# One transformer layer in fp32: dt's eight weight columns move into v's units, and the last four output tiles are shared among three engines

## The reference, cut to what matters

```
h = rms_norm(x, norm_mix_pre)
z, xbc, dt_raw, q, k, v = split(h @ w_in)        # 512, 1024, 8, 512, 512, 512 columns
dt = softplus(dt_raw + dt_bias)                  # per token and head
y_ssd = ssd_mixer(z, silu(conv(xbc)), dt, ...)   # running sums of dt * a in chunks of 128 tokens
y_diff = diff_attention(q, k, v, ...)
x = x + rms_norm(concat(y_ssd, y_diff) @ w_out, norm_mix_post)
x = x + rms_norm(cross_attention(rms_norm(x), rms_norm(mem)), norm_mem_post)
m = square(relu(rms_norm(x, norm_mlp_pre) @ w_up)) @ w_down
x = x + rms_norm(m, norm_mlp_post)
```

## Time and profile before

| | us |
|---|---|
| three runs, median (lowest to highest) | 1526.33 (1525.86 to 1528.11) |
| the profiled execution's own time | 1526.56 |
| its span | 1524.8 |
| PE busy | 1466.3 (96%) |
| DVE busy | 949.3 (62%) |
| ACT busy | 691.2 (45%) |
| GpSimd busy | 73.0 (5%) |
| HBM traffic, mean over the span | 116 GB/s |

### The profile page before, as it was taken

The page is one execution under the profiler, slowest core; times in us unless marked ns, Lnnn a source line. Parts: engine busy times, 40 slices in busy tenths (PEclk is TensorE's granted clock), DMA queues, the critical chain, the costliest instruction groups (busy, mean ns, idle before and its releaser), DMA issues. The chain is left out here.

```text
span 1524.8 us, 23241 instructions
## 1 busy us (share of the span) xinstructions
PE 1466.3 (96%) x8872; PEld 1287.9 (84%) x8872; DVE 949.3 (62%) x1658; ACT 691.2 (45%) x1473; POOL 73.0 (5%) x128
## 2 busy tenths in 40 slices
PE   7999999998998999999999989999999999999997
PEld 6889999996667999888999978888888788888885
DVE  4773465636886523711642588888777585557897
ACT  6314221225886523722642465544444464444442
POOL 1000000001001000100000234000000000000000
PEclk9999999999999999999999999999999999999999
DMA  8201111112001541011001242566443598766463
GB/s 308 65 28 42 28 29 29 29 42 84 1 1 56 160 159 43 29 56 43 14 29 56 98 135 80 180 208 219 152 152 125 195 341 285 243 227 193 155 231 110
DMA packets 99901, 177.68 MB, mean 117 GB/s; under 512 B 10576, under 2 KB 43472, under 8 KB 97744
## 3 DMA queue, kind: packets, MB, share of 16 engines
q1 hardware_dynamic: 94096, 152.05, 29.4%
q10 hardware_dynamic: 5696, 24.15, 5.0%
HBM read 138.42 MB, written 37.75 MB: 116 GB/s over the span
## 5 line engine op out<-in xcount | busy, mean ns | idle before, releaser
L1992 PE MATMUL ps<-wh,oph 128*128 128x256 f32 x1024 | 294.7, 288 | 3.2 <-DVE opl L1268 1.6
L1994 PE MATMUL ps<-wh,opl 128*128 128x256 f32 x1024 | 289.7, 283 | 0.0
L1993 PE MATMUL ps<-wl,oph 128*128 128x256 f32 x1024 | 289.7, 283 | 0.0
L1992 PEld LDWEIGHTS ps<-wh,oph 128*128 128x128 f32 x1024 | 196.2, 192 | 4.2 <-issue 2.0
L1993 PEld LDWEIGHTS ps<-wl,oph 128*128 128x128 f32 x1024 | 196.4, 192 | 0.1
L1994 PEld LDWEIGHTS ps<-wh,opl 128*128 128x128 f32 x1024 | 196.2, 192 | 0.0
L1992 PE MATMUL ps<-d_ring 128*128 128x512 f32 x448 | 174.7, 390 | 4.5 <-DVE d_ring L1877 4.5
L1993 PE MATMUL ps<-d_ring 128*128 128x512 f32 x448 | 174.4, 389 | 0.0
L1994 PE MATMUL ps<-d_ring 128*128 128x512 f32 x448 | 174.4, 389 | 0.0
L1255 DVE TENSOR_TENSOR wl<-raw,wh 128x1024 fp32r<-128x1024 f32 x60 | 73.1, 1223 | 91.8 <-ACT wh L741 91.1
L1183 ACT ACTIVATE d_ring<-left_raw 128x512 fp32r<-128x512 f32 x112 | 70.2, 627 | 98.0 <-PE ps L1994 76.9
(11 more groups left out here) (350 smaller groups left out, 2983.4 us busy)
## 6 DMA issues: line engine op xcount, KB each, us to landing
right_raw<-in_w_down_dram SPq DMA_DIRECT2D x128, 256.0 KB, 3.8
u_kept_s<-us SPq DMA_DIRECT2D x64, 256.0 KB, 2.8
left_raw<-u_kept_s SPq DMA_DIRECT2D x64, 256.0 KB, 2.9
w_blk<-in_w_up_blocks_dram ACTq DMA_DIRECT2D x14, 1024.0 KB, 6.0
left_raw<-u_kept_a SPq DMA_DIRECT2D x48, 256.0 KB, 3.1
raw<-in_w_in_dram SPq DMA_DIRECT2D x22, 512.0 KB, 3.7
u_kept_a<-u SPq DMA_DIRECT2D x24, 256.0 KB, 2.5
x_in<-in_x_dram SPq DMA_DIRECT2D x8, 512.0 KB, 9.2
```

The source lines that it names most:

```text
L1992: te.matmul(o, lh, rh, start=first, stop=False)
L1993: te.matmul(o, lh, rl, start=False, stop=False)
L1994: return te.matmul(o, ll, rh, start=False, stop=last)
```

## The change

**dt with v.** dt is no step of its own. The host lays the weights of dt and of v side by side in one tensor `w_vdt` of 520 columns, and v's two units have 260 columns each (`VC`). The slots of `wh`, `wl` and `raw` grow to 8 x 260 columns (`SLOT`). ACT evacuates each of v's first eight steps by two instructions: eight columns into `dt_tok`, 252 into `vt`. The loads, casts, products, evacuations and transposes of dt alone are gone. Softplus moves behind step n = 7 (`softplus` on ACT, `step_sizes` on DVE), the running sums to n = 10 and 11, and the SSD chunks to n = 12, 17, ..., 47. `silu_z` moves to the place of the rotary tables, so z's first step waits for `rope_done` in place of `ssd_b`, and the gate of each z tile waits for that tile's SSD output instead of all.

**The down stage.** PE waits for each of the last four chunks in turn. The multiplication of `c22_d` by the gain goes from DVE to GpSimd (`gain_last`). For tiles 4 to 6, ACT scales the second half by the tile's factor and GpSimd adds it to the residual (`finish_second`); DVE finishes the first half, one tile behind (`finish_half`). Tile 7 is finished by DVE alone. SP stores the last four tiles in halves of 512 columns, so 256 KB each.

```
-PROJ = [("xbc", 4, 4), ("dt", 2, 0), ("v", 8, 2), ("q", 8, 2), ("k", 8, 2), ("z", 8, 2),
+PROJ = [("xbc", 4, 4), ("v", 8, 2), ("q", 8, 2), ("k", 8, 2), ("z", 8, 2),
+VC = 260
+SLOT = KD * VC
-SSD_FIRST = {5 + 5 * c: c for c in range(NT)}
+SSD_FIRST = {n: c for c, n in enumerate(range(12, 12 + 5 * NT, 5))}
+C21_KEPT = {j: 16 + 2 * j + 1 for j in range(4)}
...
# SP
+            for j in range(4):
+                i, rows = 4 + j, slice((4 + j) * P, (5 + j) * P)
+                sp.wait_ge(finished, i + 1)
+                sp.dma_start(out[0][rows, 0:512], resid_d[:, i, 0:512]).then_inc(stored, 16)
+                if j < 3:
+                    sp.wait_ge(c22_p, 4 + j + 1)
+                else:
+                    sp.wait_ge(finished, NT + 1)
+                sp.dma_start(out[0][rows, 512:1024], resid_d[:, i, 512:1024]).then_inc(stored, 16)
...
# GpSimd
+            def gain_last(j):
+                pool.wait_ge(dn_kept, DN_KEPT["c22"] + j + 1)
+                g.tensor_tensor(c22_d[:, j, :], c22_d[:, j, :], gain_a[:, 512:1024], ALU.mult).then_inc(c22_p, 1)
+            def finish_second(j):
+                pool.wait_ge(dn_kept, C21_KEPT[j] + 1)
+                g.tensor_tensor(resid_d[:, 4 + j, 512:1024], c22_d[:, j, :], resid_d[:, 4 + j, 512:1024], ALU.add).then_inc(c22_p, 1)
...
+                if what == ("down", 4):
+                    for j in range(4):
+                        gain_last(j)
                 pow_step(what)
+                if what in (("down", 4), ("down", 5), ("down", 6)):
+                    finish_second(what[1] - 4)
...
# ACT, v's steps
+                    if u == 0:
+                        s.activation(dt_tok[:, i, :], ps[:, bank(g), 0:SSD_H], ACT.Copy, scale=scale).then_inc(dt_ev, 1)
+                        s.activation(vt[:, i, 0:VC - SSD_H], ps[:, bank(g), SSD_H:VC], ACT.Copy, scale=scale).then_inc(ev["v"], 1)
+                    else:
+                        s.activation(vt[:, i, VC - SSD_H:512], ps[:, bank(g), 0:VC], ACT.Copy, scale=scale).then_inc(ev["v"], 1)
...
+                if n == 7:
+                    softplus()
-                if n == 3:
+                if n == 11:
                     decays()
...
# ACT, the tail
                 s.activation(sq_d[:], c21_d[:, j, :], ACT.Square, accum_out=parts[:, j + 4, 0:1]).then_inc(dn_kept, 1)
+                if j < 3:
+                    act.wait_ge(c22_p, j + 1)
+                    act.wait_ge(rms_ready, POW[("down", j + 4)] + 1)
+                    s.activation(c22_d[:, j, :], c22_d[:, j, :], ACT.Copy,
+                                 scale=rms[:, COL[("down", j + 4)]:COL[("down", j + 4)] + 1]).then_inc(dn_kept, 1)
...
# DVE, v's steps and the tail
+                if n == 7:
+                    step_sizes()
+                if n == 11:
+                    running_sums()
+                if n == 12:
+                    chunk_ends()
...
-                    v.tensor_tensor(c22_d[:, r - 6, :], c22_d[:, r - 6, :], gain_a[:, 512:1024], ALU.mult).then_inc(gained, 1)
...
                 last_mean(j)
-                dve.wait_ge(gained, 9 + j)
-                finish(j + 4, y135_d[:, j, :], c22_d[:, j, :])
+                if j:
+                    dve.wait_ge(gained, 8 + j)
+                    finish_half(j + 3, 0, y135_d[:, j - 1, :]).then_inc(finished, 1)
+            dve.wait_ge(gained, 12)
+            finish_half(7, 0, y135_d[:, 3, :]).then_inc(finished, 1)
+            dve.wait_ge(c22_p, 4)
+            finish_half(7, 1, c22_d[:, 3, :]).then_inc(finished, 1)
...
# PE
-                if n == 0:
-                    dt_transpose()
-                if n == 3:
+                if n == 10:
                     sums_of_da()
...
-            pe.wait_ge(dn_lo, 2 * NC)
             for j in range(4):
                 for m in range(NC - ENDING, NC):
+                    pe.wait_ge(dn_lo, 2 * m + 2)
                     ins = down_chunk(m, j)
```

More of the change, by code:

```diff
@@ L647, in _ @@
                     store(m - 6 * NB - 2)
-            for i in range(4, NT):
-                store(i)
-            sp.wait_ge(stored, 16 * NT)
+            for j in range(4):
[7 more added lines that the diff above has]
+                sp.dma_start(out[0][rows, 512:1024], resid_d[:, i, 512:1024]).then_inc(stored, 16)
+            sp.wait_ge(stored, 16 * (NT + 4))
         @block.gpsimd
@@ L820, in _, with softplus @@
             silu(7)
[L821 to L829, removed]
+            def softplus():
+                act.wait_ge(small_loaded, N_SMALL)
+                act.wait_ge(dt_v, 1)
+                after(s.activation(dts[1][:], dts[0][:], ACT.Abs))
+                s.activation(dts[2][:], dts[1][:], ACT.Exp, scale=-1.0).then_inc(dt_s, 1)
+                act.wait_ge(dt_v, 2)
+                s.activation(dts[4][:], dts[3][:], ACT.Ln).then_inc(dt_s, 1)
+                s.activation(heads8[:, 1, :], heads8[:, 1, :], ACT.Exp).then_inc(dt_s, 1)
+                act.wait_ge(lam_s, 1)
+                s.activation(lam[:, 2:4], lam[:, 0:2], ACT.Exp).then_inc(dt_s, 1)
             def decays():
@@ new lines, in _, with running_sums @@
+            dt, e_cum, e_end, dt_end = dts[0], dts[4], dts[7], dts[2]
+            def running_sums():
+                dve.wait_ge(cum_done, 1)
+                cum, end = dts[5], dts[6]
+                v.tensor_copy(cum[:], ps[:, 4, 0:64].rearrange("p (c h) -> p c h", h=SSD_H)).then_inc(dv, 1)
+                v.tensor_copy(end[:], ps[:, 4, 64:128].rearrange("p (c h) -> p c h", h=SSD_H)).then_inc(dv, 1)
+                n_dv[0] += 2
+                dve.wait_ge(dv, n_dv[0])
+                after(v.tensor_scalar(ncum[:], cum[:], -1.0, None, ALU.mult))
+                v.tensor_tensor(dts[2][:], end[:], cum[:], ALU.subtract).then_inc(dt_v, 1)
@@ L1411, in heads, with chunk_ends @@
+            def chunk_ends():
+                dve.wait_ge(dt_s, 7)
+                after(v.tensor_tensor(lam[:, 4:5], lam[:, 3:4], lam[:, 2:3], ALU.subtract))
+                after(v.tensor_scalar(lam[:, 4:5], lam[:, 4:5], -LAMBDA_INIT, None, ALU.add))
+                after(v.tensor_tensor(dt_end[:], dt[:], dts[8][:], ALU.mult))
             def heads(a):
@@ L1904, in down_mean, with finish_half @@
                 mean(("down", i), D)
-            def finish(i, first, second):
+            def finish_half(i, half, part):
                 dve.wait_ge(rms_ready, POW[("down", i)] + 1)
@@ L1910, in finish @@
                 scale = rms[:, COL[("down", i)]:COL[("down", i)] + 1]
-                v.scalar_tensor_tensor(resid_d[:, i, 0:512], first, scale, resid_d[:, i, 0:512], ALU.mult, ALU.add)
-                v.scalar_tensor_tensor(resid_d[:, i, 512:1024], second, scale, resid_d[:, i, 512:1024],
-                                       ALU.mult, ALU.add).then_inc(finished, 1)
+                cut = slice(512 * half, 512 * half + 512)
+                return v.scalar_tensor_tensor(resid_d[:, i, cut], part, scale, resid_d[:, i, cut], ALU.mult, ALU.add)
+            def finish(i, first, second):
+                finish_half(i, 0, first)
+                finish_half(i, 1, second).then_inc(finished, 1)
             chunk_lo(0)
```

162 lines of the change are left out of this document (62 added, 100 removed).

## The result

The changed kernel takes 1517.31 us (median; 1513.65 to 1518.89), the kernel before, on the same chip in turns with it, 1528.11. The ratio is 0.9923 [0.9898, 0.9947]: by the ratio it is 11.8 us faster, with 8.1 to 15.6 inside the interval (the medians alone differ by 10.8). The forecast was 14.6 us less and a time of 1511.7, at most 1514.8. So the direction was right, and the median lies 2.5 us above the upper end of the range. Of the 5.6 us between 1511.7 and 1517.31, 1.8 are the kernel before, whose median was 1526.33 when the forecast was made and 1528.11 here; a range moved up by that would still end 0.7 us too low.

What follows compares the result with a forecast made beforehand. PE, busy for 96% of the span, was taken to bound the kernel, except in the tail. The terms -11.58 - 1.84 - 0.9 - 0.3 = -14.6 us took 1526.33 to 1511.7 us, range 1508.6 to 1514.8.

Steps and rivals of the forecast that it cites:

- Part A: Projections: dt's columns go into v's steps; dt's steps, transpose and a bank wait leave PE, -11.58 us in all.
- The wider product: v's 384 products: four more columns each, priced at 0.42 ns a column, +0.64 us.
- The lower end: v's 384 products: four more columns cost nothing, if a product doesn't feel them.
- The rival of a step to the price of 512 columns: v's products: 260 columns cost PE what 512 do, 41.3 us replace 0.64, ending at 1552.4 us; chance 0.03.
- 1.6 us as an upper end: v's 384 products: 4 ns more each, as dt's products showed, 1.6 us beyond the price by columns.
- B1: Last four chunks of the down stage: waits per chunk close PE's gap, -1.84 us, range -1.84 to +0.2.
- B2: Tail after PE's last products: shared among engines, DVE and GpSimd excluding each other, 13.9 us for 14.79, -0.9 us.
- The rival with no taking of turns: Tail: DVE and GpSimd don't hinder each other, tail 11.95 us, total 1509.8 us; chance 0.15.
- B3: End of the span: the last store is half as large, -0.3 us, range 0 to -0.65.

Runs made afterwards that it cites:

- e7: The changed kernel with a slot stride of 8,448 bytes and PE's operand regions moved by multiples of 256 bytes against the kernel before; 1514.1 us, ratio 0.9912.
- e2: The kernel before with only the region sizes of the changed kernel (WH and WL 16,640, RAW 8,320 bytes); 1530.68 us, ratio 1.003.
- e3: The kernel before with only dt's columns put into v's steps, SSD moved and the regions enlarged, down stage untouched; 1521.02 us, ratio 0.9955.
- e4: The kernel before with only the down stage's changes (waits per chunk, shared tail, stores by halves), region sizes untouched; 1523.37 us, ratio 0.9979.
- e11: The kernel before with only PE's wait per chunk for the last four chunks, gain products still on DVE; 1524.54 us, ratio 0.9977.
- e10: The kernel before with RAW 128 bytes larger, so that all regions behind it move by 128; 1530.29 us.
- e5: The kernel before with RAW 64 bytes larger, so that all regions behind it move by 64; 1533.15 us.
- e9: The kernel before with every buffer 128 bytes higher, so that both operands of each product move together; 1525.27 us.

## Why the prediction failed, by its steps

- **Part A, what is removed** (-11.11, -0.78, -0.33): right. With xbc's products dearer by 384 x 2.7 ns = 1.0 us and the 576 products of q, k and z that read slot 1 cheaper by 1.1 ns each (0.6), -12.2 becomes -11.8 at the attention scores, and -12.0 was measured.
- **The wider product** (+0.64, by columns): wrong and small. 260 columns take 0.1197 us, where 256 had 0.1198 before, and 0.1192 in e7. The lower end, nothing, is what holds. The rival of a step to the price of 512 columns is out.
- **The failed step: the sum has no term for where the buffers lie.** It put the effect of the larger slots and regions on all other products at nothing, without a reason. The prediction named "moving rows that begin off the present raster" as a thing that no row shows, took the dearer dt products (0.2315 us) as its price, and laid it on v's 384 products alone, 1.6 us as an upper end. The hint was right and the place was wrong: v's products don't feel it, but 512-column products do, in stages that the diff doesn't touch, because `WH`, `WL` and `RAW` push all that lies behind. By the traces: xbc 384 x 2.7 ns = 1.0 us, mq 384 x 2.9 = 1.1, t2 to t4 576 x 6.1 = 3.5, the up stage's other 768 products 0.7, the down stage 0.4, and 1.9 back from 256-column products: +4.8 us. e2 shows the regions' part of it without any other edit (4.6 us, 3.1 to 6.3), e3 that part A alone brings it (-12.2 + 4.8 = -7.4, for -6.9 measured), e7 that it can be had back.
- **B1** (-1.84): right. The gap is gone in e4, e11 and the changed kernel, and none has a wait for the last chunk. GpSimd's gain products cost DVE 1.1 us, at the one split that the prediction named (0.3 to 1.5), and no wait of PE came of it.
- **B2** (-0.9): right in its mechanism and mis-sized by 0.3, 14.16 us for 13.9, so -0.63. The rival with no taking of turns (11.95) is out.
- **B3** (-0.3): DVE's end to the span's end is 2.6 us for 3.0, -0.4. A store of 256 KB lands 2.2 us after its issue, one of 512 KB 2.6; no run shows a transfer's own moving time, by which the term was estimated.

With +4.8 for the places, nothing for 0.64, -0.63 and -0.4 for B2 and B3, the sum is -15.1 + 4.8 = -10.3 us, and 0.7 more come from the wait at the start of the down stage: the landmarks' -11.0. That it closes to 0.1 us is luck, since the attention alone varies by more. The measured ratio (-8.1 to -15.6) holds both this and, just, the forecast's own difference; the traces decide between them, with an up stage that is 4.1 us longer in every kernel that has the new places and in none that hasn't.

What stays open: why the operands' places against each other matter in this way; why products of 256 columns, with the moving operand in slot 1, are 1.1 ns cheaper instead of dearer (0.1186 us for 0.1198); why the surplus reaches three products beyond a block with 128 bytes and ten with 64; and what other spacings cost in a long run of products. Dt's 0.2315 us, by which the prediction priced its upper end, is no riddle of width: it is a mean over rows at eight offsets.

## What to carry to other kernels

When a buffer grows, every product whose operands lie on either side of it has them at another spacing: count region sizes as part of the change, keep them and the strides inside at multiples of 256 bytes, and compare the mean start-to-start distance of the matrix products stage by stage, also in stages that the diff leaves alone. Four more columns on 256 cost nothing here, where dt in steps of its own, with the tokens as the moving operand, took 48 products of 512 columns. And before work is handed to GpSimd beside DVE, make the schedule with both taking turns; here DVE alone ends 1.4 us earlier.

## What the runs showed of the hardware

- A 512-column float32r product takes 0.2267 us when its operands' starts are congruent modulo 256 bytes (shifts of 0, 256 and 1,024). At 128 bytes apart it takes 0.2333 in a long block, at 64 bytes 0.2289 (e10, e5). If both move by 128 it is 0.2267 again (e9).
- A switch costs as well: behind a block with 128 bytes the next three products, whose own operands didn't move, take 0.2317 us, and behind one with 64 bytes the next ten take 0.2316. Rows of single products mislead there: in a block of the changed kernel the distances alternate between 0.2375 and 0.2292 us. Means over a block, with the block behind it, don't.
- The granted clock between 350 and 500 us, where PE has short idle times (16 of 150 us), was 0.95 to 0.99 in thirteen executions of nearly the same work, and the attention took 115.6 to 119.5 us with it.
- 256 and 260 columns cost the same to 0.7 ns, 0.1192 to 0.1199 us.
- A one-element power on GpSimd is held from 0.54 to 0.99 us beside one DVE instruction that reads two SBUF tiles, and a DVE mean of one element from 0.16 to 0.53 (1504.87 in the changed kernel) beside GpSimd's addition.
